# Score tiles in two banks by turns, attention's small pieces joined between products, and a later gating order in a hybrid decoder block

## What is computed

```python
z = q @ k.T * d**-0.5                      # stick-breaking attention, strictly causal
w = exp(log_sigmoid(z) + sum of log_sigmoid(-z) over the later keys)
u_sb = ((w @ v) * silu(sb_z)) @ w_sb_proj
S_t = diag(f_t) S_{t-1} + k_t v_t^T ;  o_t = S_t^T q_t        # HGRN2, in chunks
u_hg = (rmsnorm(o) * silu(hg_z)) @ w_hg_proj
out = rmsnorm(x + (gate_sb * u_sb + gate_hg * u_hg) @ w_out)
```

## Time and profile before

| | |
|---|---|
| median of 3 runs | 1419.0 us (1418.84 to 1419.8) |
| the profiled execution, its own time | 1419.46 us |
| its span, first to last instruction | 1417.7 us |
| PE busy | 1346.7 us (95%) |
| DVE, POOL, ACT busy | 937.0, 721.8, 585.8 us |
| mean granted TensorE clock | 0.978 of full |
| chain that ended last, share of the span | PE 77%, POOL 6%, DVE 5%, ACT 5%, issue 4%, DMA 3% |

### The profile page before, as it was taken

One profiled execution on the slowest core, in us unless ns is written; L12 is line 12 of the kernel. 1 busy time (PEld: TensorE's weight loads), 2 busy tenths in 40 slices (PEclk: granted clock), 3 DMA queues, 4 the chain that ended last, 5 costly groups with the idle time before them and its releaser, 6 DMA issues.

```text
span 1417.7 us, 23087 instructions
## 1 busy us (share of the span) xinstructions
PE 1346.7 (95%) x8408; PEld 1119.7 (79%) x8408; DVE 937.0 (66%) x1066; ACT 585.8 (41%) x966; POOL 721.8 (51%) x488
## 2 busy tenths in 40 slices
PE   5679999999999999999999999999989889999998
PEld 4568878888878878878888888887877668888886
DVE  4827976976986886797696697787544446545323
ACT  8326346345435625625634633553344321201131
POOL 6655754565555554574466456554488612223210
PEclk8799999999999999999999999999999989999999
DMA  5121121111211121112111211114334465434502
GB/s 149 30 75 31 61 74 46 61 31 60 73 48 60 31 90 60 31 61 90 30 61 45 74 62 31 60 44 145 135 123 164 149 200 178 155 93 124 199 31 104
DMA packets 134350, 119.41 MB, mean 84 GB/s; under 512 B 10097, under 2 KB 116593, under 8 KB 134257
## 3 DMA queue, kind: packets, MB, share of 16 engines
q1 hardware_dynamic: 125040, 92.84, 20.9%
q10 hardware_dynamic: 9216, 25.17, 5.1%
HBM read 88.63 MB, written 29.36 MB: 83 GB/s over the span
## 4 chain that ended last, share of the span: by engine, by line
PE 77%; POOL 6%; DVE 5%; ACT 5%; issue 4%; DMA 3%; ACTq 0%; SPq 0%; DVEq 0%; POOLq 0%
PE banks L1529 41%; PE banks L1780 12%; PE banks L1802 6%; PE banks L1610 5%; PE banks L1586 4%; POOL b_lo L592 3%; POOL b_sum L592 2%; PE banks L1600 2%; PE banks L1669 1%; ACT b_hi L682 1%; DMA w_raw<-in_w_in 1%; DVE hk L1052 1%; PE banks L1644 1%; PE banks L1671 1%; PE banks L1664 1%
## 5 line engine op out<-in xcount | busy, mean ns | idle before, releaser
L1529 PE MATMUL banks<-a_hi,b_hi 128*128 128x512 f32 x1120 | 465.3, 415 | 33.9 <-DVE a_lo L1052 10.7
L1529 PE MATMUL banks<-a_hi,b_lo 128*128 128x512 f32 x1120 | 443.5, 396 | 0.0
L1529 PE MATMUL banks<-a_lo,b_hi 128*128 128x512 f32 x1120 | 442.6, 395 | 0.0
L592 POOL TENSOR_TENSOR b_lo<-w_raw,b_hi 128x512 fp32r<-128x512 f32 x108 | 171.4, 1598 | 247.6 <-ACT b_hi L682 247.6
L1529 PEld LDWEIGHTS banks<-a_hi,b_hi 128*128 128x128 f32 x1120 | 213.9, 191 | 79.5 <-issue 24.8
L592 POOL TENSOR_TENSOR b_lo<-b_sum,b_hi 128x512 fp32r<-128x512 f32 x120 | 173.7, 1448 | 154.6 <-ACT b_hi L682 154.6
L1529 PEld LDWEIGHTS banks<-a_hi,b_lo 128*128 128x128 f32 x1120 | 213.5, 191 | 48.1
L1529 PEld LDWEIGHTS banks<-a_lo,b_hi 128*128 128x128 f32 x1120 | 214.6, 192 | 37.7
L1154 DVE TENSOR_TENSOR_SCAN kappa<-kappa 128x128 f32<-128x128 f32 (+3 forms) x64 | 96.1, 1502 | 100.6 <-ACT kappa L799 100.6
L682 ACT ACTIVATE b_hi<-b_sum 128x512 fp32r<-128x512 f32 x120 | 75.7, 632 | 156.6 <-POOL b_sum L592 156.4
L666 POOL TENSOR_TENSOR w_lo<-w_raw,w_hi 128x1024 fp32r<-128x1024 f32 x20 | 49.0, 2456 | 155.2 <-ACT w_hi L682 155.2
(11 more groups left out here) (194 smaller groups left out, 2516.1 us busy)
## 6 DMA issues: line engine op xcount, KB each, us to landing
w_raw<-in_w_in SPq DMA_DIRECT2D x72, 512.0 KB, 4.9
gate_d<-gate_out SPq DMA_DIRECT2D x16, 512.0 KB, 3.0
gate_in<-gate_d ACTq DMA_DIRECT2D x32, 256.0 KB, 2.9
x_tok<-in_x SPq DMA_DIRECT2D x8, 512.0 KB, 6.4
z_d<-z_out SPq DMA_DIRECT2D x8, 512.0 KB, 2.7
hz_d<-z_out SPq DMA_DIRECT2D x8, 512.0 KB, 2.7
osb_d<-o_sb SPq DMA_DIRECT2D x8, 512.0 KB, 5.9
ohg_d<-hq SPq DMA_DIRECT2D x8, 512.0 KB, 2.6
```

What stands on the lines that cost most here:

```text
L592: return nc.gpsimd.tensor_tensor(dst, a, b, op)
L1529: last = mm(bank, w[:, s, k, :], t[s][:, k, :], start=opens and k == 0 and z == 0, stop=k == QUAD - 1 and z == 2, skip_group_check=not opens)
```

## The change

The schedule of a half head is written anew, scores of j < 4 use banks 4 and 5 by turns, the values, the turn and the scores of a point stand in this order behind the point's products, ACT takes every turned part behind `pair_point`, and tile order and times of the gating change. Cut: only renamed arguments and the equal edits of `osb_low` and `osb_gate` are left out.

```diff
-TURN_AT = {3: (0, 0), 5: (1, 0), 7: (2, 0), 9: (3, 0), 12: (4, 0), 13: (4, 1), 15: (5, 0), 16: (5, 1),
-           18: (6, 0), 19: (6, 1), 21: (7, 0), 22: (7, 1)}
-PV_AT = {4: 0, 6: 1, 8: 2, 10: 3, 14: 4, 17: 5, 20: 6, 23: 7}
-FINISH_AT = {10: 0, 23: 1}
+TURN_AT = {4: (0, 0), 6: (1, 0), 8: (2, 0), 11: (3, 0), 13: (4, 0), 14: (4, 1), 16: (5, 0), 17: (5, 1),
+           19: (6, 0), 20: (6, 1), 22: (7, 0), 23: (7, 1)}
+PV_AT = {6: 0, 8: 1, 11: 2, 13: 3, 16: 4, 19: 5, 22: 6, 24: 7}
+FINISH_AT = {13: 0, 24: 1}
-OSB_FETCHED = {1: (0,), 2: (1, 2), 3: (3,), 4: (4,), 5: (5,), 7: (6, 7)}
-OSB_GATED = {2: (0,), 3: (1, 2), 4: (3,), 5: (4,), 6: (5,), 7: (6, 7)}
+OSB_FETCHED = {(1, 3): (0,), (2, 3): (2, 3), (3, 1): (1,), (3, 5): (4,), (4, 3): (5,), (7, 3): (6, 7)}
+OSB_TIMES_Z = {2: (0,), 3: (2, 3), 4: (1,), 5: (4,), 6: (5,), 7: (6, 7)}
+OSB_GATED = {3: (0,), 4: (2, 3), 5: (1,), 6: (4,), 7: (5, 6, 7)}
+OSB_ORDER = (0, 2, 3, 1, 4, 5, 6, 7)
 def score_banks(j):
     n_banks = 1 if j < 4 else 2
-    return n_banks, (j + 1) * P // n_banks
+    return 4 + (j % 2 if j < 4 else 0), n_banks, (j + 1) * P // n_banks
...
# ScalarE, second_half
-                    if u in TURN_AT and TURN_AT[u][1] == 0:
-                        take_turned(h, *TURN_AT[u])
                     pair_point(pair, n, p)
-                    if u == PAIR_POINTS + 9:
-                        act.wait_ge(product_done, PRODUCTS * n + P2 + 1)
-                        act.wait_ge(pv_done, 8 * h + 8)
-                        take_c11(pair, turn_in)
...
-                    if u in TURN_AT and TURN_AT[u][1] == 1:
+                    if u in TURN_AT:
                         take_turned(h, *TURN_AT[u])
...
                     if u in FINISH_AT:
                         finish_sb(h, FINISH_AT[u])
+                        if FINISH_AT[u] == 1:
+                            take_c11(pair, turn_in)
...
# ScalarE, gate pairs
-                    if p == 3:
-                        if g == 1:
+                    for e in OSB_FETCHED.get((g, p), ()):
+                        if e == 0:
                             act.wait_ge(sb_stored, 16 * HEADS)
                             act.wait_ge(z_stored, 16 * 2 * HEADS)
-                        if g == 2:
+                        if e == 1:
                             act.wait_ge(hg_stored, 16 * HEADS)
...
-                    for order, e in enumerate(OSB_GATED.get(g, ())):
-                        if p == (7, 9)[order]:
+                    if p == 9:
+                        for e in OSB_TIMES_Z.get(g, ()):
                             osb_sigmoid(e)
-                        if p == (11, 12)[order]:
+                    if p == 7 and not final:
+                        for e in OSB_GATED.get(g, ()):
                             osb_high(e)
+                    if final and p in (7, 11, 12):
+                        osb_high({7: 5, 11: 6, 12: 7}[p])
...
                     act.wait_ge(ohg_step, 2 * t + 1)
+                    act.wait_ge(ohg_sig_done, t + 1)
                     fetch_ohg(t + 2)
...
# VectorE, gate pairs 2 to 7
                 take_u2(n, n)
-                osb_multiply(here[0])
+                for e in OSB_GATED.get(g, ())[:1 if last_pair else None]:
+                    osb_gate(e)
                 take_u3(n, n)
-                for e in here[1:]:
+                for e in OSB_TIMES_Z[g]:
                     osb_multiply(e)
                 dve.wait_ge(gate_stored[1], 16 * g)
                 take_c22(GATE_PAIR, n)
-                for e in here:
-                    osb_gate(e)
+                for e in OSB_GATED.get(g, ())[:1 if last_pair else None]:
+                    osb_low(e)
+                if last_pair:
+                    for e in OSB_GATED[g][1:]:
+                        osb_gate(e)
                 take_c12(GATE_PAIR, n)
-                for e in here:
-                    osb_low(e)
+                if last_pair:
+                    for e in OSB_GATED[g][1:]:
+                        osb_low(e)
...
# VectorE, branch panels
             for t in range(KT):
-                split_ohg(t)
+                if t > 0:
+                    split_ohg(t - 1)
+                if t == KT - 1:
+                    split_ohg(t)
                 gate_sb(t, 0)
                 gate_sb(t, 1)
...
# TensorE, scores
-                else:
-                    pe.wait_ge(sig_done, 8 * h + j)
-                n_banks, m = score_banks(j)
+                elif j > 1:
+                    pe.wait_ge(sig_done, 8 * h + (j - 1 if j < 4 else j))
+                bank, n_banks, m = score_banks(j)
...
# TensorE, second_half
-                    if u in TURN_AT and TURN_AT[u][1] == 0 and TURN_AT[u][0] >= 4:
-                        turn(h, *TURN_AT[u])
                     project(pair, 4 * h + pair, u % PAIR_POINTS)
                     if u == V_AT:
                         turn_values(h)
-                    if u in TURN_AT and not (TURN_AT[u][1] == 0 and TURN_AT[u][0] >= 4):
+                    if u in PV_AT:
+                        attend_sb(h, PV_AT[u])
+                    if u in TURN_AT:
                         turn(h, *TURN_AT[u])
                     if u in QK_AT:
                         scores(h, QK_AT[u])
-                    if u in PV_AT:
-                        attend_sb(h, PV_AT[u])
```

More of the change, by code:

```diff
@@ L791, in sigmoids @@
                 act.wait_ge(qk_done, 8 * h + j + 1)
-                n_banks, m = score_banks(j)
-                score = banks[:, 4:4 + n_banks, 0:m]
+                bank, n_banks, m = score_banks(j)
+                score = banks[:, bank:bank + n_banks, 0:m]
                 def keys(t):
@@ L927, in osb_sigmoid @@
             def osb_sigmoid(e):
-                act.wait_ge(osb_times_z, e + 1)
+                act.wait_ge(osb_times_z, OSB_ORDER.index(e) + 1)
                 nc.scalar.activation(osb_z[e][:, :], osb_z[e][:, :], ACT.Sigmoid).then_inc(osb_sig_done, 1)
             def osb_high(e):
-                act.wait_ge(osb_gated, e + 1)
+                act.wait_ge(osb_gated, OSB_ORDER.index(e) + 1)
                 copy(osb_hi[e][:, :], osb_raw[e][:, :]).then_inc(osb_hi_ready, 1)
@@ L970, in _ @@
                         make_gate(g, 1, slice(0, S), gate_out[1][:, :]).then_inc(gate_made[1], 1)
-                    if p == 3:
-                        if g == 1:
+                    for e in OSB_FETCHED.get((g, p), ()):
+                        if e == 0:
                             act.wait_ge(sb_stored, 16 * HEADS)
                             act.wait_ge(z_stored, 16 * 2 * HEADS)
-                        if g == 2:
+                        if e == 1:
                             act.wait_ge(hg_stored, 16 * HEADS)
-                        if final:
+                        if e == 6:
                             act.wait_ge(product_done, done + P1 + 1)
-                        for e in OSB_FETCHED.get(g, ()):
-                            fetch_osb(e)
-                    for order, e in enumerate(OSB_GATED.get(g, ())):
-                        if p == (7, 9)[order]:
+                        fetch_osb(e)
+                    if p == 9:
+                        for e in OSB_TIMES_Z.get(g, ()):
                             osb_sigmoid(e)
-                        if p == (11, 12)[order]:
+                    if p == 7 and not final:
+                        for e in OSB_GATED.get(g, ()):
                             osb_high(e)
+                    if final and p in (7, 11, 12):
+                        osb_high({7: 5, 11: 6, 12: 7}[p])
                     if final and p == 8:
@@ L1400, in osb_gate @@
             def osb_gate(e):
-                dve.wait_ge(osb_sig_done, e + 1)
+                dve.wait_ge(osb_sig_done, OSB_ORDER.index(e) + 1)
                 tt(osb_raw[e][:, :], osb_raw[e][:, :], osb_z[e][:, :], ALU.mult).then_inc(osb_gated, 1)
             def osb_low(e):
-                dve.wait_ge(osb_hi_ready, e + 1)
+                dve.wait_ge(osb_hi_ready, OSB_ORDER.index(e) + 1)
                 tt(osb_lo[e][:, :], osb_raw[e][:, :], osb_hi[e][:, :].bitcast(F32), ALU.subtract).then_inc(osb_split, 1)
@@ L1450, in _ @@
                 n += 1
-                here = OSB_GATED[g]
+                last_pair = g == N_GATE_PAIRS - 1
                 take_u2(n, n)
-                osb_multiply(here[0])
+                for e in OSB_GATED.get(g, ())[:1 if last_pair else None]:
+                    osb_gate(e)
                 take_u3(n, n)
-                for e in here[1:]:
+                for e in OSB_TIMES_Z[g]:
                     osb_multiply(e)
@@ L1580, in scores @@
                     need(pe, on_done, 2 * h)
-                else:
-                    pe.wait_ge(sig_done, 8 * h + j)
-                n_banks, m = score_banks(j)
+                elif j > 1:
+                    pe.wait_ge(sig_done, 8 * h + (j - 1 if j < 4 else j))
+                bank, n_banks, m = score_banks(j)
                 for c in range(n_banks):
```

(6 more changed lines are left out.)

## The result

The changed kernel takes 1430.1 us in the median of 7 runs (1424.2 to 1436.4), the kernel before 1419.5 (1418.3 to 1422.7) on the same chip: ratio 1.0074, 95% interval 1.0054 to 1.0094, so 7.7 to 13.3 us slower. Forecast were 1422.5 in a range of 1406 to 1432, with 0.48 for slower. The profiled execution took 1430.27 us, its span is 1428.5, 10.8 more than before.

What follows compares the result with a forecast made beforehand. Heads taken as a PE-bound stream where only idle stretches count: heads +12.2, clock +6, gate pairs -6.8, branch panels -6.7, last head -1.2, sum +3.5 over 1419.46, less 0.46: 1422.5 us. Own range 1418 to 1427; with rivals 1406 to 1432.

Steps and rivals of the forecast that it cites:

- The walk through ACT's order: Heads, points 19 to 24: turn (7, 1)'s copy behind P6's rounding makes PE wait 2.5 us in each of eight heads.
- X + 9.8: Heads, u = 24: PE reaches block 7's values 9.8 us after leaving turn (6, 0) at X; ACT's copy is ready at X + 12.3.
- u = 17: Heads, first new wait: PE's turn (5, 1) needs the bank ACT still copies, 0.5 us lost a head (0 to 1.2).
- The scores' 1.41 a head: Heads, block 1: scores no longer wait for ACT's sigmoids, 1.41 us gained in each of seven heads.
- Heads together: All eight heads: seven times +1.6 (+11.2) and head 0 +1.0, in all +12.2 us, without the clock.
- The last head's term: Last head: hands its smaller wait for gate_out, 1.6 us, to the first gate pair; -1.2 us (0 to -2).
- The clock: Heads, behind the 2.5 us wait: granted clock falls in four of eight at 1.5 us each, +6 us (0 to 19).
- Joined pieces: Half heads, small pieces at 16 points instead of 20: taken as 0, at most 0.05 us each, 1.6 us in all.
- below 0.3: Heads: by the skill's 216 ns a matmul, PE would reach the new wait below 0.3 us a head earlier and lose as much more.
- The gate pairs: Gate pairs: ACT rounds some 5 us earlier, so POOL's waits and a clock fall go; -6.8 us (-3 to -9).
- The rival in which the gating's gain does not come: Gate pairs: DVE's longer stretch ahead of take_c22 makes a new wait in each pair; 1429.5 us, chance 0.10.
- The branch panels: First branch panels: 4.6 us of wait and a clock fall of 2.4 go, 0.3 back at t = 7; -6.7 us (-4 to -7.5).

Runs made afterwards that it cites:

- the head without waits: Changed kernel with ACT's copy of turn (7, 1) ahead of pair_point at u = 23 and hq's sigmoid behind the copy of turn (5, 0): 1400.5 us (0.9859).
- the one-bank kernel: Changed kernel with turn (7, 1)'s copy ahead of pair_point, hq's sigmoid at u = 16, and scores of j < 4 all in bank 4 again: 1413.8 us (0.9952).

## Why the prediction was right, and where not

**What decided is as predicted.** The walk through ACT's order gave 2.5 us of wait at u = 24 (1.1 to 3.9); measured 2.82, or 2.99 from start to start as the 2.5 was counted, and undoing that one order gives 25 us back. PE's side of the walk came out as said (X + 9.8). ACT and POOL were 0.5 late: from the end of P1's rounding to T6 9.15 us went by instead of 8.67, of which POOL's first pass makes 0.50 (1.78 at 602.97, before 1.28). Why that pass is slower is not shown. At u = 17 it gave 0.5; measured 0.31, or 0.48 from start to start. The scores' 1.41 a head and 3.8 left in head 0 at the turn: 3.9. Heads together were +12.2 and 6 for the clock, less 1.2 at the last head; measured on the chip +16.8. That close a sum is partly luck: eight waits 0.5 longer (4), joined pieces better by 0.2 a head (1.8) and one fall of the clock fewer (1.5) largely cancel. The last head's term held: its wait of 1.61 for `gate_out` is 0.49.

**The clock**: four falls of 1.5 in eight heads were forecast, and the profile has three, of 1.5. That was a guess between two rows and is not more than that: 2.8 us lies where it goes either way, and the changed kernel's runs spread over 12 us where those before spread over 4. That the number of falls differs between runs is likely: the mean granted clock is 0.986 in the fastest run (1424.2) and 0.977 and 0.980 in the two slowest (1434.9, 1436.4). The falls themselves were seen in one run only.

**Joined pieces** were put at 0 with a bound of 0.2 a head. Before less 1.41 is 112.78 and the head without waits takes 112.54; the one-bank kernel is 0.22 under before. So some 0.2 a head, the upper bound. Joined places and other positions were not tried apart. By the Trainium skill, "TensorE: Matmul & The Clock Gate", section "Back-to-back issue gap", the gap of a single matmul of 512 columns is about 216 ns, and in a sustained stream one takes about 131 ns; by either the new wait would be longer. The trace keeps 0.23 us (609.64 to 610.10 in two steps), near the first. By the Trainium skill's 216 ns the 30 matmuls ahead of the wait would take 0.4 us less, an estimate; the prediction's "below 0.3" was counted too low.

**The gate pairs are the step that failed**: -6.8 forecast, measured -0.4 to -2.5. The prediction let the 4.5 and the clock's 2.4 go because ACT would round 5 us earlier. It named no work that is late next in pair 3 beyond 0.4. Two tiles fetched at pair 2 are four DMAs, issued now ahead of SP's output store, weight loads and gate store; with these the gate store took 8.2 us (6.6 before) and ACT waited 4.30 us for it. The prediction counted the moved DMAs against what ACT waits for and not against what they delay. The result, with 1406 to 1432 around it, lies above the forecast's own 1418 to 1427, for this and for what the branch panels gave less. The rival in which the gating's gain does not come (0.10, at 1429.5) has the outcome, but its cause, DVE's stretch ahead of `take_c22`, made at most the 1.80 in pair 4; in pair 3 it was the store.

**The branch panels**: -6.7, measured about -3.5. From the end of pair 7's wait on, the changed kernel's trace is 3.6 shorter than before, that of the panels' edit alone 5.6. The wait left, 2.4 forecast, is 1.95 in the first and 1.72 in the second. Behind 1.95 the granted clock fell again (0.67 in the 5 us from 1166), which the sum excluded although it held a fall behind 2.5 us possible elsewhere; behind 1.72 it held. In both 1.24 came back at panel 7, not 0.3. The cause of that is in the timelines of POOL and DVE there:

```profile
1236.71 3.05 POOL L670 TENSOR_TENSOR w_lo<-w_raw,w_hi 128x1024 fp32r<-128x1024 f32 x1 [5.95 <-ACT w_hi L686]
...
1237.53 2.77 DVE L1421 CAST ohg_hi<-ohg_raw 128x1024 fp32r<-128x1024 f32 x1
...
1243.99 0.70 DVE L1421 CAST ohg_hi<-ohg_raw 128x1024 fp32r<-128x1024 f32 x1
```

The same cast takes 2.77 while POOL's subtraction runs and 0.70 when it doesn't; so it does at panel 7 of every kernel here with this order, and no other cast of the branch panels takes more than 0.70. The two tiles, put at 10 us, took 10.9 (1235.02 to 1245.87), and 8.8 is twice the second tile's 4.4.

The sum came out 7.6 below the median. Of this the gates and panels make 7.2 (13.5 of gain forecast, 6.3 measured) and the kernel before 0.5 (1419.0 in the forecast, 1419.5 beside the changed kernel); the heads, 17.0 forecast with the last head's term and 16.8 measured, take 0.2 back.

## What to carry to other kernels

A wait that costs nothing is harmless only by what stands behind it. Before moving a piece past an instruction on an in-order engine, list that engine's waits, the harmless ones too, and ask of each who would wait for the moved piece. And a wait removed is worth the distance to the next one, not its own length: two banks alone gave 0 of 1.4 us a head, later turns alone 0.2, both 1.65.

## What the runs showed of the hardware

Behind idle stretches of PE of 2.8 us (2.68 in head 0) the granted clock fell to 0.50 in three of eight heads, with 3.86 (3.72) in eight of eight, at 1.5 and 2.3 us a fall; behind 1.24 us never in the heads. Elsewhere it fell behind 1.80, 1.95 and 2.55 us and held behind 1.61, 1.72 and 2.21. The one kernel with 2.8 us in every head is also uneven from run to run (12 us against 4). And a DVE cast of 128x1024 took four times as long, 2.77 against 0.70 us, beside a POOL subtraction.
